# Gate and up partly by seven block products for eight, in three passes a layer

## The reference, cut to what matters

```python
def swiglu(h, w_gate, w_up, w_down):
    return (jax.nn.silu(h @ w_gate) * (h @ w_up)) @ w_down
...
        x = x + swiglu(rms_norm(x, ffn_norm[l]), w_gate[l], w_up[l], w_down[l])
```

## Time and profile before

| | us |
|---|---|
| three runs | 1770.68, 1771.25, 1771.81 |
| median | 1771.25 |
| span of the profiled execution, first to last instruction | 1769.1 |
| TensorE busy in it | 1761.5 |
| VectorE, ScalarE, GpSimd busy in it | 1130.7, 914.3, 113.1 |

### The profile page before, as it was taken

The page is one execution under the profiler, slowest core; times in us unless marked ns, Lnnn a source line. Parts: engine busy times, 40 slices in busy tenths (PEclk is TensorE's granted clock), DMA queues, the critical chain, the costliest instruction groups (busy, mean ns, idle before and its releaser), DMA issues.

```text
span 1769.1 us, 29325 instructions
## 1 busy us (share of the span) xinstructions
PE 1761.5 (100%) x10438; PEld 1564.0 (88%) x10438; DVE 1130.7 (64%) x1460; ACT 914.3 (52%) x1176; POOL 113.1 (6%) x132
## 2 busy tenths in 40 slices
PE   9999999999999999999999999999999999999998
PEld 6888888888888888889999888888888888888887
DVE  5766666556666666678997776666655566666554
ACT  6666664334444453456775466666533344445433
POOL 2100000000000001124111420000000000000000
PEclk9999999999999999999999999999999999999999
DMA  7555556545555566545445555555665455556642
GB/s 282 195 188 190 189 197 229 191 155 177 190 190 190 190 223 196 175 152 160 148 137 179 190 184 191 189 188 188 230 200 166 162 190 190 190 190 222 227 146 72
DMA packets 86017, 328.79 MB, mean 186 GB/s; under 512 B 9680, under 2 KB 11088, under 8 KB 85840
## 3 DMA queue, kind: packets, MB, share of 16 engines
q1 hardware_dynamic: 85680, 327.03, 55.5%
q10 hardware_dynamic: 288, 1.11, 0.2%
HBM read 326.01 MB, written 2.10 MB: 185 GB/s over the span
## 4 chain that ended last, share of the span: by engine, by line
PE 100%; DVE 0%; issue 0%; DVEq 0%; ACT 0%; POOL 0%; POOLq 0%
PE ps L435 58%; PE ps L436 31%; PE ps L505 2%; PE ps L443 1%; PE ps L445 1%; PE ps L444 1%; PE ps L799 1%; PE ps L798 1%; PE ps L797 1%; PE ps L633 0%; PE ps L632 0%; PE ps L631 0%; PE ps L685 0%; PE ps L493 0%; PE ps L705 0%; PE ps L706 0%
## 5 line engine op out<-in xcount | busy, mean ns | idle before, releaser
L1238 DVE TENSOR_TENSOR w_lo<-raw,w_hi 128x1024 fp32r<-128x1024 f32 (+2 forms) x564 | 736.0, 1308 | 419.1 <-ACT w_hi L850 416.9
L435 PE MATMUL ps<-xg,w_hi 128*128 128x512 f32 x2880 | 999.7, 390 | 0.0
L850 ACT ACTIVATE w_hi<-raw 128x1024 fp32r<-128x1024 f32 (+2 forms) x565 | 630.9, 1120 | 548.9 <-PE ps L436 533.2
L436 PE MATMUL ps<-xg,w_lo 128*128 128x256 f32 x2880 | 812.1, 282 | 0.0
L435 PEld LDWEIGHTS ps<-xg,w_hi 128*128 128x128 f32 x2880 | 540.5, 188 | 113.5 <-DVE w_lo L1238 0.3
L436 PEld LDWEIGHTS ps<-xg,w_lo 128*128 128x128 f32 x2880 | 544.3, 189 | 0.1
L435 PE MATMUL ps<-act,w_hi 128*128 128x512 f32 x1320 | 458.0, 390 | 0.0
L436 PE MATMUL ps<-act,w_lo 128*128 128x256 f32 x1320 | 372.2, 282 | 0.0
L435 PEld LDWEIGHTS ps<-act,w_hi 128*128 128x128 f32 x1320 | 247.7, 188 | 51.9
L436 PEld LDWEIGHTS ps<-act,w_lo 128*128 128x128 f32 x1320 | 249.5, 189 | 0.0
L1318 DVE TENSOR_TENSOR sums<-ps,cross 128x512 f32<-128x512 f32 x88 | 60.8, 691 | 93.1 <-ACT cross L928 93.1
(11 more groups left out here) (200 smaller groups left out, 1240.2 us busy)
## 6 DMA issues: line engine op xcount, KB each, us to landing
raw<-w_gate SPq DMA_DIRECT2D x176, 512.0 KB, 3.2
raw<-w_up SPq DMA_DIRECT2D x176, 512.0 KB, 3.2
raw<-w_down SPq DMA_DIRECT2D x120, 704.0 KB, 4.2
raw<-w_o SPq DMA_DIRECT2D x32, 512.0 KB, 3.2
raw<-w_last SPq DMA_DIRECT2D x11, 512.0 KB, 3.2
raw<-w_q_a SPq DMA_DIRECT2D x8, 512.0 KB, 3.2
raw<-w_kv_a SPq DMA_DIRECT2D x8, 512.0 KB, 3.3
raw<-w_q_nope SPq DMA_DIRECT2D x8, 512.0 KB, 3.2
```

The source lines that it names most:

```text
L435: pe.matmul(ps[:, bank, :], w_hi[:, s, j * P:(j + 1) * P], moving, start=start, stop=False)
L436: return pe.matmul(ps[:, bank, 0:SEQ], w_lo[:, s, j * P:(j + 1) * P], moving[:, 0:SEQ], start=False, stop=stop)
L850: nc.scalar.activation(dst, src, ACT.Copy).then_inc(hi_ready, 1)
L1238: nc.vector.tensor_tensor(lo, src, hi.bitcast(F32), ALU.subtract).then_inc(lo_ready, 1)
```

## The change

The FFN of a layer runs in three passes of 16, 14 and 14 feature tiles (`PASS_TILES`), each with its down product after it. In a pass, two or three groups (`PASS_GROUPS`) of two feature tiles each are computed by Strassen's scheme on 2 x 2 blocks: tokens in two halves of 128, k in two halves of 8 tiles, features in two tiles, where gate and up of one feature tile stand beside each other as 256 columns. Seven block products, named P1 to P7, take the place of eight. A group's product runs in two chunks of four k-tiles (`group_chunk`): the activations are stationary, high, high and low, and the split weights move, 256 columns in each of three matmuls.

The weight operands are the quarters W11, W12, W22 and W21 of the group, two chunks each, loaded into ring slots 0 to 7, and sums of them. VectorE adds W12 to W11 behind the split of P1, and W22 to that behind the split of P5 (`split_up`, `add_quarter`). GpSimd adds W22 to W12, and the sum in W11 to W21, by DMAs from `raw` to `raw` that accumulate (`group_sums`). So a group has 8 loads, 14 splits and 8 additions, four of them by DMA. The activation operands are four sums and differences of token and k blocks, made once a layer in steps 4 to 13 of its first pass by VectorE and ScalarE (`mix_step`), with ring slots 4 to 7 as scratch. The results of a group are tokens by features; they are combined, gated and multiplied there with a row factor by token, and turned by four transposes on TensorE (`turn_parts`) before they are split into `act`. For these row factors the statistics product also makes sums by token (two products of two columns).

All other feature tiles are computed as before, now with three raw slots of their own. `up_order` writes out the order of a pass: 20 or 4 plain chunks ahead, the group chunks with plain ones strewn in, 7 plain chunks at the end. In pass 0 the first group's chunks stand at steps 20, 21 (P1), 23, 25 (P5), 27, 28 (P6), with plain chunks at 22, 24 and 26; in pass 1 at 4, 5 (P1), 7, 8 (P5), 10, 11 (P6), plain ones at 6 and 9. In step k VectorE and ScalarE do what the end of chunk k allows and then split chunk k + 4. `up_loads` writes out SP's order, sorted by the step at which a slot comes free; in pass 0 it runs ... plain 16, plain 17, W22 (two), W21 (two), plain 18, plain 19 ..., and in pass 1 plain 0 to 2, the eight quarters of the first group, plain 3. Loops over the chunks of gate and up are written out.

```diff
+PASSES = 6
+LAYER_PASSES = PASSES // 2
+PASS_TILES = (16, 14, 14, 16, 14, 14)
+PASS_GROUPS = (2, 3, 3, 2, 3, 3)
+PASS_LEAD = (20, 4, 4, 20, 4, 4)
+PASS_TAIL = 7
+MIX_STEPS = 14
+FH = PASS_TILES[-1]
+RING_SLOTS = 8
+PLAIN_SLOTS = 3
...
+PRODUCTS = ("P1", "P5", "P6", "P2", "P7", "P3", "P4")
+QUARTERS = ("W11", "W12", "W22", "W21")
+READS = {"P1": "W11", "P5": "W11", "P6": "W11", "P2": "W21", "P7": "W12", "P3": "W22", "P4": "W21"}
+def up_order(q):
+    groups = PASS_GROUPS[q]
+    seven = [("S", g, r, c) for g in range(groups) for r in PRODUCTS for c in range(2)]
+    plain = [("P", p, c) for p in range(PASS_TILES[q] - 2 * groups) for c in range(4)]
+    lead, tail = PASS_LEAD[q], PASS_TAIL
+    order, mixed, done = plain[:lead], plain[lead:len(plain) - tail], 0
+    for k, s in enumerate(seven):
+        order.append(s)
+        upto = (k + 1) * len(mixed) // len(seven)
+        order += mixed[done:upto]
+        done = upto
+    return order + plain[len(plain) - tail:]
+UP_ORDER = [up_order(q) for q in range(PASSES)]
...
+def freed_by(g, w, c):
+    return GROUP_AT[g, {"W11": "P2", "W12": "P7", "W22": "P3", "W21": "P4"}[w], c]
+def wanted_by(g, w, c):
+    return GROUP_AT[g, {"W11": "P1", "W12": "P1", "W22": "P5", "W21": "P2"}[w], c]
+def up_loads(q):
+    loads = []
+    for k, s in enumerate(UP_ORDER[q]):
+        n = CHUNK[UPS[q]] + k
+        if s[0] == "P":
+            before = PLAIN_NO[n] - PLAIN_SLOTS
+            free = PLAIN_AT[before] if before >= 0 else 0
+            loads.append((max(free, CHUNK[UPS[q]] - 1), n, ("chunk", n)))
+    for g in range(GROUPS_BEFORE[q], GROUPS_BEFORE[q + 1]):
+        for w in QUARTERS:
+            for c in range(2):
+                free = freed_by(g - 1, w, c) + (3 if w == "W11" else 0) if g > GROUPS_BEFORE[q] else 0
+                if free == 0 and q % LAYER_PASSES == 0 and w in ("W22", "W21"):
+                    free = CHUNK[UPS[q]] + MIX_STEPS
+                loads.append((max(free, wanted_by(g, w, c) - 24, CHUNK[UPS[q]] - 1), wanted_by(g, w, c),
+                              ("quarter", g, w, c)))
+    return [load for _, _, load in sorted(loads, key=lambda x: x[:2])]
...
+            def load_plain(n):
+                s, before = raw_slot(n), PLAIN_NO[n] - PLAIN_SLOTS
+                if before >= 0:
+                    sp.wait_ge(lo_ready, made(PLAIN_AT[before]))
+                sp.dma_start(raw[:, s, :], w_plain[PLAIN_NO[n]]).then_inc(landed[s], 16)
+            def load_quarter(q, g, w, c):
+                s = quarter_slot(w, c)
+                if g > GROUPS_BEFORE[q]:
+                    if w == "W11":
+                        sp.wait_ge(fourth_sum[c], 16 * g)
+                    else:
+                        sp.wait_ge(lo_ready, made(freed_by(g - 1, w, c)))
+                else:
+                    if q == 0:
+                        sp.wait_ge(chunks_used, s + 1)
+                    else:
+                        n = CHUNK[UPS[q]] - 1
+                        sp.wait_ge(lo_ready, made(n - (n - s) % RING_SLOTS))
+                    if q % LAYER_PASSES == 0 and w in ("W22", "W21"):
+                        sp.wait_ge(mix_ready, 4 * (q // LAYER_PASSES + 1))
+                row = (g * len(QUARTERS) + QUARTERS.index(w)) * 2 + c
+                sp.dma_start(raw[:, s, :], w_group[row]).then_inc(landed[s], 16)
...
+            def group_chunk(q, k):
+                _, number, r, c = UP_ORDER[q][k]
+                n, g = CHUNK[UPS[q]] + k, GROUPS_BEFORE[q] + number
+                s = n % SPLIT_SLOTS
+                pe.wait_ge(lo_ready, made(n))
...
+                for j in range(KTS):
+                    kt = c * KTS + j
+                    if r in MIXES:
+                        x_hi, x_lo = (mix_hi_lo[:, MIXES.index(r), kt, part, :] for part in range(2))
+                    else:
+                        first = P if r == "P4" else 0
+                        of = kt if r == "P1" else TILES + kt
+                        x_hi, x_lo = (xg[:, of, part * SEQ + first:part * SEQ + first + P] for part in range(2))
+                    wh, wl = (w[:, s, j * WIDE:(j + 1) * WIDE] for w in (w_hi, w_lo))
+                    pe.matmul(dst, x_hi, wh, start=(kt == 0 and r in ("P1", "P5")), stop=False,
+                              skip_group_check=True)
+                    pe.matmul(dst, x_hi, wl, start=False, stop=False, skip_group_check=True)
+                    mm = pe.matmul(dst, x_lo, wh, start=False, stop=(kt == TILES - 1),
+                                   skip_group_check=True)
+                mm.then_inc(chunks_used, 1)
...
+            def turn_parts(g):
...
+                for k, at in enumerate((0, 3, 1, 2)):
+                    mm = pe.transpose(ps[:, STATS, k * P:(k + 1) * P], part[:, at, P:], const[:, C_IDENT:C_IDENT + P])
+                mm.then_inc(part_turned, 1)
...
-                with pe.Fori(0, FH // 2 - peel) as i:
-                    for f in range(4):
-                        long_tile(n0 + BODY * peel + 2 * f, t0 + 4 * peel + f, xg, TILES, i, 4)
+                for k in range(begin, len(UP_ORDER[q])):
+                    if stats is not None and k == 5:
+                        sum_over_partitions(stats, by_rows=True)
+                    g = ended(q, k - 4, "P4")
+                    if g is not None:
+                        turn_parts(g)
+                    if UP_ORDER[q][k][0] == "P":
+                        plain_chunk(q, k)
+                    else:
+                        group_chunk(q, k)
...
+            def add_quarter(g, w, c, done):
+                src, dst = quarter_slot(w, c), quarter_slot("W11", c)
+                ve.wait_ge(landed[src], 16 * LOAD_NO["quarter", g, w, c])
+                nc.vector.tensor_tensor(raw[:, dst, :], raw[:, dst, :], raw[:, src, :], ALU.add).then_inc(done, 1)
+            def split_up(n):
+                split(n)
+                step = up_step(n)
+                if step is None or step[0] == "P":
+                    return
+                g = GROUPS_BEFORE[up_pass(n)] + step[1]
+                if step[2] == "P1":
+                    add_quarter(g, "W12", step[3], first_sum)
+                elif step[2] == "P5":
+                    add_quarter(g, "W22", step[3], second_sum)
...
+            def corner(q, slot, kt, s):
+                col = (G_FFN0, G_FFN1)[q // LAYER_PASSES] + kt
+                of = x[:, kt:kt + TILES, s * P:(s + 1) * P]
+                step(nc.vector.tensor_tensor(mixed_raw(slot), of, gain[:, col:col + TILES, :].broadcast_to([P, TILES, P]),
+                                             ALU.mult))
...
+            def mix_sum(q, number, dst, a, b, op):
+                nc.vector.tensor_tensor(mixed_raw(dst), mixed_raw(a), mixed_raw(b), op).then_inc(mix_summed, 1)
+                ve.wait_ge(mix_summed, 4 * (q // LAYER_PASSES) + number + 1)
+            def mix_low(q, number):
+                at, src, sign = ((0, 7, 1.0), (2, 6, 1.0), (1, 4, -1.0), (3, 5, 1.0))[number]
+                ve.wait_ge(mix_hi, 4 * (q // LAYER_PASSES) + number + 1)
+                nc.vector.scalar_tensor_tensor(mix_hi_lo[:, at, :, 1, :], mixed_raw(src), sign,
+                                               mix_hi_lo[:, at, :, 0, :].bitcast(F32),
+                                               ALU.mult, ALU.subtract).then_inc(mix_ready, 1)
+            def mix_step(q, k):
+                if k == 4:
+                    ve.wait_ge(chunks_used, CHUNK["up0"])
+                    corner(q, 4, 0, 0)
+                elif k == 5:
+                    corner(q, 6, 0, 1)
...
+                elif k == 9:
+                    mix_sum(q, 2, 4, 4, 7, ALU.add)
+                    mix_low(q, 0)
+                elif k == 10:
+                    corner(q, 5, TILES, 0)
+                    mix_low(q, 1)
...
+                elif k == MIX_STEPS - 1:
+                    mix_low(q, 3)
...
+            def add_quarter(into, of, c, done):
+                gp.dma_start(raw[:, quarter_slot(into, c), :], raw[:, quarter_slot(of, c), :],
+                             accum_op=ALU.add).then_inc(done, 16)
+            def group_sums(q):
+                for g in range(GROUPS_BEFORE[q], GROUPS_BEFORE[q + 1]):
+                    for c in range(2):
+                        gp.wait_ge(second_sum, 2 * g + c + 1)
+                        add_quarter("W12", "W22", c, third_sum[c])
+                    for c in range(2):
+                        gp.wait_ge(lo_ready, made(GROUP_AT[g, "P2", c]))
+                        add_quarter("W21", "W11", c, fourth_sum[c])
```

More of the change, by code:

```diff
@@ new lines, with load_numbers @@
+UP_LOADS = [up_loads(q) for q in range(PASSES)]
+def load_numbers():
+    numbers, count, order = {}, [0] * (RING_SLOTS + PLAIN_SLOTS), []
+    for n in range(CHUNK["end"]):
+        q = up_pass(n)
+        if q is None:
+            order.append(("chunk", n))
+        elif n == CHUNK[UPS[q]]:
+            order += UP_LOADS[q]
+    for load in order:
```

(50 more changed lines are left out.)

520 lines of the change are left out of this document (387 added, 133 removed).

## The result

The changed kernel takes 1774.80 us (median of 18 runs), the kernel before 1771.37 in the same job: a ratio of 1.0018, with a 95% interval of 1.0011 to 1.0026. One of the 18 runs took 8636.94 us, for a reason that no trace shows; the ratio leaves it out, and without it the median is 1774.75. The forecast was 1769.0, 0.13% under the median that it knew. So the time lies in the forecast's own range (1758 to 1778), but it moved the other way: by 3.4 us, which is just inside the 3.5 that the prediction calls no change, and yet clear of the noise, since the interval does not hold 1. The profiled execution took 1774.95 us, 1.85 more than its span.

The account below looks back on a forecast made before the run. TensorE's own work bounds the kernel. Span: 1769.1 - 36.1 + 7.0 + 0.7 = 1740.7, then + 21.4 + 4.1 + 0.6 = 1766.8; with 2.15 above span, forecast 1769.0 us, own range 1758 to 1778, full range 1747 to 1797.

Parts of the forecast that it names:

- The saving on TensorE: Gate and up groups: 168 matmuls at 0.1186 us save 2.26 a group, 36.1 us over 16; four transposes each add 7.0.
- The hole at chunk 18: Passes 0 and 3: plain chunk 18's load stands behind quarters awaiting the mixed sums; TensorE waits 9.2 us a layer.
- The rival without a hole: Passes 0 and 3: mixing done sooner or load not held back, 21.4 us not spent, 1747.6; chance 0.20.
- what follows the hole: Passes 0 and 3: TensorE without lead at the first group's adds waits 1.5 us more (0.6 chunk 22, 0.9 chunk 24).
- The angles in pass 1: Start of pass 1: VectorE's rotary angles delay the first group's work, so TensorE waits for chunk 9, +4.1 us.
- Passes 2, 4 and 5: Start of these passes: the same strip has a down stage's lead and comes out level, 0.2 us each, +0.6.
- The DMA sums: Weight sums by DMA: 4.5 us each, hidden under 16 us of cover; rival says they come late, 1801, chance 0.14.
- VectorE as the bound amid the groups: Short passes: VectorE owes 35.4 of 39.7 us a group, costed nothing; rival adds 44 us, 1813, chance 0.13.

Follow-up runs that it names:

- Experiment six: Changed kernel with mixing spread, first group's quarters listed singly between plain loads, and rotary angles in pass 0's last four down tiles: 1746.50 us, 0.9858 of the kernel before.
- experiments two: Changed kernel with unread products filling TensorE's wait ahead of plain chunk 18 in passes 0 and 3: 1773.53 us, 1.0012 of the kernel before.
- four: Changed kernel with mixing one operation a chunk, 24 plain chunks ahead, quarters W22 and W21 behind plain chunk 22: 1762.11 us, 0.9950 of the kernel before.
- five: As experiment four, but W22's and W21's quarters listed one at a time between plain loads: 1750.87 us, 0.9886 of the kernel before.
- experiment three: Changed kernel with the rotary angles moved into VectorE's last four down tiles of pass 0: 1770.36 us, 0.9993 of the kernel before.
- experiment seven: As experiment six, but the third and fourth weight sums made by VectorE instead of DMAs: 1763.08 us, 0.9955 of the kernel before.
- experiment one: Changed kernel with the first group's W22 and W21 quarters listed behind plain chunks 18 and 19 in passes 0 and 3: 1760.79 us, 0.9941 of the kernel before.

## Why the prediction was wrong, point by point

**The saving on TensorE** was right. The products of a group go at 0.118 to 0.119 us, and a turn of four transposes takes 0.35 and makes the next matmul start 0.09 late, 0.44 as said. In pass 1 (start, length):

```profile
378.54 0.60 PE L817 MATMUL ps<-const,part 128*128 128x128 f32 x4
378.89 0.48 PE L634 MATMUL ps<-xg,w_hi 128*128 128x512 f32 x1
379.21 0.28 PE L635 MATMUL ps<-xg,w_lo 128*128 128x256 f32 x1
...
381.75 0.28 PE L802 MATMUL ps<-w_hi,mix_hi_lo 128*128 128x256 f32 x1
...
384.59 0.39 PE L634 MATMUL ps<-xg,w_hi 128*128 128x512 f32 x1
```

(24 starts from 381.75 to 384.59: 0.1183 each, against the 0.1186 taken from the earlier trace rows.) Experiment six shows the whole sum, as good as without waits: 1745.1 less its one of 0.9 is 1744.2, against 1740.7 reckoned, 3.5 more. Of that, 0.8 lies ahead of the statistics product, which starts at 56.83 in six (57.15 in the changed kernel) and at 56.03 before, in the pool stage: its 64 matmuls (L708) take a mean 611 ns in six (617 in the changed kernel), where they took 596 before. The change is not shown to be the cause, since they take 596 in experiments two, four and five as well. The rest, 2.7, lies in the two layers' FFNs, and no run tells its parts apart.

**The hole at chunk 18** was right in each link. Measured from the statistics product at 57.1, the sums were ready after 35.4 us (35.1 predicted), chunk 18 after 47.7 (46), and TensorE waited 9.4 in four pieces (9.2 predicted). In pass 3 the sums took 35.4 as well and chunk 18 46.5, but TensorE waited 6.7: it came 1.6 us later to chunk 18, since its clock was low at 1077 to 1084.6 (0.22 of 7.6 us is 1.7), and the chunk came 1.2 sooner. Two small slips in the prediction's sums change nothing: 512 KB at 408 GB/s are 1.29 us and not 1.31, and chunk 3 lands 1.0 us into pass 1 and not 1.1. The rival without a hole is thereby out.

**The step that failed is what follows the hole:** "It comes out without lead, just when the first group's four extra adds fall due: I reckon 1.5 more". No such wait came, though it does in experiment four, where the clock stays at 1.00 behind the long wait of pass 3 (0.5, 0.6 and 0.9). In its place TensorE ran behind the long waits at a granted 0.50 and 0.69, which costs 2.4 (0.50 of 4.7 us) and 1.6 us (0.31 of 5.0). I had counted a wait at its own length, and TensorE at its full pace on both sides of it: refilling and low clock stood in the sum at nothing, without a reason given, and were 9.2 us together. Experiment two shows that the lost lead and the low clock are partly one: of the 4.0 us, 1.3 come back as waits for VectorE, and about 1 is gained (0.9 by the traces from the statistics product on, 1.3 by the medians).

**The difference in the sum,** 1773.1 - 1766.8 = 6.3 us of span, is thus made of one term that helped and three that leaned the other way. The waits were 20.0 us, less than the 26.1 predicted (-6.1: 3.0 of lost lead that did not come, 2.5 in pass 3, and 0.6 for the other passes); refilling behind 13 of them at 0.27 (+3.5) and low clock (1.7 in the middle of pass 3, 2.4 and 1.6 behind the long waits: +5.7) were not in it; and the work itself is put longer by the 3.5 that six shows. That makes 6.6. No term is large, but the forecast stood 0.13% from no change, and they were enough for the other sign: without the 9.2 us of refilling and low clock the span would have been 1763.9, under the 1769.1 before. The chance of "slower" had been given nearly all to rivals that did not come; what came was the forecast's own mechanism with a dearer wait.

**The angles in pass 1** cost 4.1 us of span by experiment three, as predicted, but by luck in part: the five waits of pass 1 are 3.9 us, and four of them, 3.0, are the angles'; the other 1.1 is refilling, which the sum did not have. VectorE starts the fifth chunk's low part at 331.18, after the angles, as in the earlier trace rows. **Passes 2, 4 and 5** have no wait, where 0.6 was put.

**The DMA sums** at nothing: right. They land in

```profile
DMA to landing us min/median/max: 4.5/5.8/9.5
```

(L2208, 64 of them), all under the 16 us of cover, and ScalarE never waits for one. The 4.5 taken was their minimum, and their median of 5.8 is still far from 16. The queues' rows at the top give what an adding transfer costs the engines: 11.0% of the span for 33.56 MB is 0.33% a MB, 53.2% for 327.03 MB of loads 0.16%. By the Trainium skill (Collectives: The Full Stack, The bandwidth ceiling), which says of the adding transfers of a reduce-scatter that they read two sources and so run at half the rate of a copy, it would be twice, and the trace agrees: 2.0 times. No plain copy within SBUF runs here, so that part of the factor lies in the other source is not ruled out.

**VectorE as the bound amid the groups** did not come about, but it is near: four additions more a group, experiment seven, cost 17 us. The prediction's reckoning (35.4 of 39.7 us) was sound.

## What to carry to other kernels

A load that waits for something late must not stand ahead of loads that don't, in a list that is taken in order; four of them at once hold up the next one (it was copied 8.1 us after its issue in the changed kernel, 9.1 in experiment four), which costs nothing only where chunks made ready in advance cover it, as in experiment one; so space them. One-time work of a side engine is best put where that engine has spare time chunk by chunk: spreading the mixing, with its loads spaced, and moving the angles returned 13.5 us of span here (1758.6 to 1745.1) with not one instruction less on TensorE. And where the engine that sets the time waits, the wait is not the whole price: add the refilling and the granted clock of the stretch behind it, and ask whether a low clock only hides that another engine is late.

## What the runs showed of the hardware

That a wait of TensorE can cost more than its length was not expected here: after 6.3 us of standing the granted clock was 0.50 for 4.7 us, and with products that keep TensorE at work in the wait it was 1.00, in pass 3 even though 2.3 us of the wait were left. The length of a wait alone did not decide: in experiment four the clock fell behind 2.9 us in pass 0 (0.62 at 111 to 115) and stayed at 1.00 behind 3.7 us in pass 3. Short waits were not all alike: the same 0.8, 0.5 and 1.8 us left the clock at 1.00 in pass 0 of the changed kernel (90 to 98.5), and took it to 0.78 in pass 3 of it, to 0.72 in pass 3 of experiment one and to 0.80 in pass 0 of experiment two.

The Trainium skill (TensorE: Matmul & The Clock Gate, A second HAM failure mode) tells of a kernel whose clock goes down and up because TensorE pauses briefly and often between groups of matmuls; the 0.78 after three short waits agrees with it, and the 1.00 after the same three shows that it need not happen each time.
